# Four 32x32 blocks in place of two masked 64x64 blocks in the level steps of a blocked triangular inverse

## What is computed

```python
def step(S, inp):
    r_t, w_t, k_t, v_t, a_t, b_t = inp
    sa = jnp.einsum('bhvk,bhk->bhv', S, a_t)
    S = S * w_t[:, :, None, :] + sa[..., None] * b_t[:, :, None, :] + v_t[..., None] * k_t[:, :, None, :]
    y = jnp.einsum('bhvk,bhk->bhv', S, r_t)
    return S, y
```

## Time and profile before

| | |
|---|---|
| time, median of 3 runs | 3553.84 us (3550.99 to 3561.1) |
| the profiled execution's own time | 3547.82 us |
| its span, first to last instruction | 3546.0 us |
| `rw_core`, about | 1590 to 2045 us of the span |
| one turn of `m`, about | 57 us |

### The profile page before, as it was taken

One profiled execution on the slowest core, in us unless ns is written; L12 is line 12 of the kernel. 1 busy time (PEld: TensorE's weight loads), 2 busy tenths in 40 slices (PEclk: granted clock), 3 DMA queues, 4 the chain that ended last, 5 costly groups with the idle time before them and its releaser, 6 DMA issues. The chain is left out here.

```text
span 3546.0 us, 61071 instructions
## 1 busy us (share of the span) xinstructions
PE 3405.1 (96%) x25028; PEld 2748.4 (78%) x25028; DVE 1984.6 (56%) x2398; ACT 1194.9 (34%) x1597; POOL 1590.5 (45%) x1148
## 2 busy tenths in 40 slices
PE   7998999999999999999999999999999999999989
PEld 5886778888888777888787877888888887674767
DVE  6886565556224652226767647555542458868452
ACT  4654233333102362226465524333310231242221
POOL 3442377775333323334344425877633323560352
PEclk9998999999999999999999999999999999999999
DMA  2111122224311142241212211222332113111212
GB/s 103 48 49 38 33 87 79 80 89 152 109 42 56 40 179 95 95 147 39 85 46 86 68 37 48 88 89 78 111 128 88 52 42 119 61 48 42 101 43 76
DMA packets 74063, 274.58 MB, mean 77 GB/s; under 512 B 8208, under 2 KB 8592, under 8 KB 73360
## 3 DMA queue, kind: packets, MB, share of 16 engines
q1 hardware_dynamic: 68112, 250.79, 20.8%
q10 hardware_dynamic: 5760, 20.97, 1.5%
HBM read 207.77 MB, written 63.96 MB: 77 GB/s over the span
## 5 line engine op out<-in xcount | busy, mean ns | idle before, releaser
L117 POOL TENSOR_TENSOR gap<-ones 128x1 f32<-128x1 f32 x150 | 46.0, 307 | 1238.8 <-PE ps L167 774.4
L120 POOL TENSOR_TENSOR wlo<-wraw,whi 128x1024 fp32r<-128x1024 f32 (+3 forms) x150 | 391.6, 2611 | 12.5
L893 DVE TENSOR_TENSOR h<-ps,h 128x1024 f32<-128x1024 f32 (+1 forms) x56 | 68.5, 1223 | 288.9 <-PE ps L416 259.6
L167 PE MATMUL ps<-xh,whi 128*128 128x512 f32 x640 | 203.0, 399 | 21.6 <-ACT rw_stage L1888 5.1
L167 PE MATMUL ps<-xl,whi 128*128 128x512 f32 x640 | 199.2, 393 | 0.0
L167 PE MATMUL ps<-xh,wlo 128*128 128x512 f32 x640 | 198.7, 392 | 0.0
L1007 POOL TENSOR_TENSOR wlo<-wraw,whi 128x512 fp32r<-128x512 f32 x126 | 166.3, 1335 | 52.6 <-ACT whi L1130 52.6
L118 POOL TENSOR_SCALAR whi<-wraw 128x1024 fp32r<-128x1024 f32 (+3 forms) x150 | 178.9, 1192 | 0.0
L384 ACT ACTIVATE sq<-h 128x1024 f32<-128x1024 f32 x32 | 34.0, 1061 | 394.1 <-DVE h L893 304.0
L2200 POOL TENSOR_TENSOR rw_levels<-rw_levels,rw_masks 128x512 f32<-128x512 f32 x64 | 87.2, 1378 | 177.2 <-PE ps L2289 140.8
L167 PEld LDWEIGHTS ps<-xh,whi 128*128 128x128 f32 x640 | 119.7, 190 | 56.6 <-issue 8.9
(11 more groups left out here) (673 smaller groups left out, 9535.0 us busy)
## 6 DMA issues: line engine op xcount, KB each, us to landing
wraw<-w_ffn_in SPq DMA_DIRECT2D x88, 512.0 KB, 3.5
ffn_hidden<-sum_of_squares SPq DMA_DIRECT2D x44, 512.0 KB, 2.6
rw_next<-rw_kept SPq DMA_DIRECT2D x40, 512.0 KB, 5.1
wraw<-w_ffn_out SPq DMA_DIRECT2D x32, 512.0 KB, 3.6
ffn_stage<-ffn_hidden SPq DMA_DIRECT2D x30, 512.0 KB, 4.9
rw_kept<-rw_stage SPq DMA_DIRECT2D x24, 512.0 KB, 2.7
rw_kept<-rw_stage ACTq DMA_DIRECT2D x24, 512.0 KB, 2.7
wraw<-w_ple SPq DMA_DIRECT2D x16, 640.0 KB, 3.8
```

Source lines behind the costliest of these rows:

```text
L117: nc.gpsimd.tensor_tensor(g.gap[:, 0:1], g.ones[:, 0:1], g.ones[:, 0:1], ALU.mult)
L120: nc.gpsimd.tensor_tensor(g.wlo[:, s, 0:w], g.wraw[:, s, 0:w], g.whi[:, s, 0:w].bitcast(F32), ALU.subtract).then_inc(g.w_split.sem, 1)
L167: last = nc.tensor.matmul(acc[:, hf, :], w[:, s, c:c + P], x[:, kt, hf * HALF:(hf + 1) * HALF], start=start and kt == 0 and n == 0, stop=s ...
L893: nc.vector.tensor_tensor(ht, flat(banks(g, acc + 2 * s)), ht, ALU.add).then_inc(g.acc_free.sem, 1)
```

## The change

In the levels 2 to 16, every 64x64 matmul becomes two 32x32 matmuls on the array's diagonal. Since a 32-block couples only to itself in these levels, the masks need only 32 columns: the mask work reads `Nc` once and writes 128x256. `Nm` becomes a list of two buffers of that size in the same memory, used in turn, and the mask of a level now waits for the correction of two levels before. `X` is kept 32 columns wide in levels 2 to 16, with one copy instead of two. The last level is as it was. The table of masks shrinks from 834 to 706 columns.

```diff
-NARROW = ["same"] + [f"off{b}" for b in LEVELS] + ["strictT", "inclT", "eye"]
+NARROW = ["same", "strictT", "inclT", "eye"]
 BLOCK_AT = len(NARROW) * CH
-GROUP_AT = BLOCK_AT + 2 * BLK
+GROUP_AT = BLOCK_AT + (2 + len(LEVELS)) * BLK
...
-    Nm = by_tile(level[:, 1, :])
+    Nm = [by_tile(level[:, 1, n * HALF:(n + 1) * HALF]) for n in (0, 1)]
...
-            for lev, b in enumerate(LEVELS):
+            for lev in range(LAST):
                 for h in (0, 1):
-                    if lev == 0:
+                    if lev < 2:
                         pool.wait_ge(g.nc_ready.sem, g.nc_ready.base + m + 1)
                     else:
-                        pool.wait_ge(g.x_done.sem, g.x_done.base + 2 * LEV * m + 2 * (lev - 1) + h + 1)
-                    nc.gpsimd.tensor_tensor(halved(Nm[:, h]), twice(Nc[:, h]), mask_wide(f"off{b}"), ALU.mult).then_inc(g.off_ready.sem, 1)
+                        pool.wait_ge(g.x_done.sem, g.x_done.base + 2 * LEV * m + 2 * (lev - 2) + h + 1)
+                    nc.gpsimd.tensor_tensor(Nm[lev % 2][:, h], Nc[:, h], mask_level(lev), ALU.mult).then_inc(g.off_ready.sem, 1)
...
             for j in range(NT):
-                for rows in heads:
-                    last = nc.tensor.matmul(block_bank(X_BANK + h)[rows, j, :], Nm[rows, h, j, :], DTc[rows, h, j, :], start=True, stop=True)
+                for rows in quarters:
+                    last = nc.tensor.matmul(block_bank(X_BANK + h)[rows, j, :], Nm[lev % 2][rows, h, j, :], DTc[rows, h, j, :], start=True, stop=True)
...
             for j in range(NT):
-                for rows in heads:
-                    last = nc.tensor.matmul(block_bank(D_BANK + h)[rows, j, :], X[rows, h, j, :], D[rows, h, j, :], start=True, stop=True)
+                for rows in quarters:
+                    last = nc.tensor.matmul(block_bank(D_BANK + h)[rows, j, :], X[rows, h, j, 0:BLK], D[rows, h, j, :], start=True, stop=True)
...
         def keep_correction(m, lev, h):
             act.wait_ge(g.x_done.sem, g.x_done.base + 2 * LEV * m + 2 * lev + h + 1)
-            ins = nc.scalar.activation(X[:, h, :, 0:BLK], block_bank(X_BANK + h), ACT.Copy, scale=upper)
             if lev < LAST:
-                ins = nc.scalar.activation(X[:, h, :, BLK:CH], block_bank(X_BANK + h), ACT.Copy, scale=lower)
+                ins = nc.scalar.activation(X[:, h, :, 0:BLK], block_bank(X_BANK + h), ACT.Copy)
+            else:
+                ins = nc.scalar.activation(X[:, h, :, 0:BLK], block_bank(X_BANK + h), ACT.Copy, scale=upper)
             ins.then_inc(g.x_ready.sem, 1)
```

More of the change, by code:

```diff
@@ L1594, in mask_constants @@
     t, s = np.meshgrid(np.arange(P) % CH, np.arange(CH), indexing="ij")
-    off = lambda b: (t // (2 * b) == s // (2 * b)) & (t // b % 2 == 1) & (s // b % 2 == 0)
     m = {"same": t // BLK == s // BLK, "strictT": t < s, "inclT": t <= s, "eye": t == s}
-    m.update({f"off{b}": off(b) for b in LEVELS})
     r, c = np.meshgrid(np.arange(P) % BLK, np.arange(BLK), indexing="ij")
-    block = [(r // 2 == c // 2) & (r % 2 == 1) & (c % 2 == 0), r == c]
+    off = lambda b: (r // (2 * b) == c // (2 * b)) & (r // b % 2 == 1) & (c // b % 2 == 0)
+    block = [off(1), r == c] + [off(b) for b in LEVELS]
     upper = np.arange(P)[:, None] // BLK % 2 == 0
@@ L2084, in rw_core @@
     mask_block = lambda n: mk[:, BLOCK_AT + n * BLK:BLOCK_AT + (n + 1) * BLK].rearrange("p (o s) -> p o s", o=1).broadcast_to([P, 2 * NT, BLK])
+    mask_level = lambda lev: mk[:, BLOCK_AT + (2 + lev) * BLK:BLOCK_AT + (3 + lev) * BLK].rearrange("p (o s) -> p o s", o=1).broadcast_to([P, NT, BLK])
     mask_wide = lambda n: narrow(n).rearrange("p o (a s) -> p o a s", a=2).broadcast_to([P, NT, 2, BLK])
```

## The result

The changed kernel takes 3642.48 us, the median of 5 runs (3637.91 to 3650.37), against 3550.99 us (3550.01 to 3561.1) for the one before: ratio 1.0257, 95% interval 1.0245 to 1.0268. It is 91 us slower; 64 us on the median were forecast, in the range 3576 to 3664. The profiled execution has a span of 3636.9 us. Outside `rw_core` nothing moved: the stretch up to 1590 us and the 1502 us behind the core are as long as before.

What follows compares the result with a forecast made beforehand. TensorE's pace was taken to bound the levels, with instruction fetch binding after the change: 3547.8 + 66 us (8.2 us a turn, 8 turns) = 3614 us profiled. With the median 6 us above, it said 3618 us, range 3576 to 3664.

Steps and rivals of the forecast that it cites:

- What bounds the kernel: TensorE's own pace in the levels; instruction fetch in `outputs` and `gram`, 256 instructions lasting at least about 3.65 us.
- Removals at nothing: One ScalarE copy in 64 places (0.47 us) and half GpSimd's mask work (from 1.38 us) count as nothing.
- Pace of four blocks at once: Array time of a 32x32 level call: 1.0 us at 16 ns a record, or half of that; neither taken.
- Changes of block size: Some 14 changes a turn, about 0.1 us each, 0 to 1.4 us a turn; taken as 0.
- The sum: Per turn, 3.6 us plus 4.6 us added in the two dense level stretches, 8.2 us; 8 turns, 66 us.
- first part: `gram_ar` to `key_sum`: 448 more instructions, 1259 in all, 16.4 us against about 12.8, plus 3.6 us a turn.
- second part: `key_sum`, one call and `variance`, 4.7 us: 144 instructions, less than a block, nothing added.
- third part: Levels 8, 16 and last: 512 more instructions, 1281 in all, 16.6 us against 12.0, plus 4.6 us a turn.
- the upper bound that the prediction gave it: Fetch cost with nothing left of a block at the start and 3.9 us a block: 10 us a turn, 80 in all.
- the rule: Dense stretch: first 128 instructions about 1 us, each block entered 3.65 us, last part some 1.9 us a whole block.
- The clock's rival: Clock falls a level earlier, taking `key_sum` and `variance` with it: up to 32 us more, around 3650 us; chance 0.14.
- The room of 2048 instructions: Would let TensorE hold several blocks in the levels, so fetch doesn't bind: 3506 us; chance 0.07.

Runs made afterwards that it cites:

- `e1_pairs`: Changed kernel with 16 matmuls in place of 32 in each call of levels 2 to 16, same 32x32 blocks, half the products wrong: 3525.5 us, ratio 0.9942.
- `e8_fillall`: Changed kernel with one fp32 128x128 filler matmul on 256 columns ahead of each of the 20 calls of a turn: 3652.6 us, ratio 1.0299.
- `e7_relief`: Kernel before, matmuls untouched, with one ScalarE copy and masks of 32 columns in levels 2 to 16 from the second turn on: 3545.9 us, ratio 0.9982.
- half of the change: Kernel before with `inverses` alone in 32x32 blocks and one ScalarE copy in levels 2 to 16: 3582.7 us, ratio 1.0094.
- `e3_fill`: Changed kernel with two fp32 128x128 filler matmuls on 256 columns ahead of each call of levels 2 and 4: 3646.6 us, ratio 1.0274.
- padding runs: Kernel before with 16 tiny matmuls ahead of each call of levels 2 to 16: on one block 3747.1 us; spread over four blocks 3679.2 us.
- `e10_warm`: Kernel before with one fp32 128x128 filler matmul ahead of each of the last level's four calls a turn: 3552.4 us, ratio 0.9998.
- `e2b_pad4`: Kernel before with 16 tiny matmuls, spread over the four 32x32 diagonal blocks, ahead of each call of levels 2 to 16: 3679.2 us, ratio 1.0356.

## Why the prediction held, and where its sum was small

- **What bounds the kernel.** Right: before, the array's pace and the supply of instructions lie close together in the levels; after, the supply rules. The 123 packets, their distance and the blocks of 256 between rests came as written, and halving the count (`e1_pairs`) took the whole loss away. Putting 88 us of the array's work into seven turns made them 2.5 us shorter (`e8_fillall`), so the array isn't what they wait for in the levels.
- **Removals at nothing.** Right to within 6 us (`e7_relief`).
- **Pace of four blocks at once.** The faster bound: 128 records in 1.46 - 0.19 us, 10 ns each, at full clock. None of it reached the time. Changes of block size cost nothing that shows: the run with half the count has them all and is faster than before.
- **The sum.** The mechanism was right and terms were mis-sized. Mean over the first seven turns, from line to line: first part 12.7 to 17.7 us, plus 5.0 (3.6 forecast); second 4.6 to 5.8, plus 1.2 (0); third 11.9 to 17.4, plus 5.4 (4.6); the rest of the turn minus 0.5 (0). In all 11.2 a turn, 90 us, against 8.2 and 66. The supply's share, 9.9 a turn or 80 us, is the upper bound that the prediction gave it; the 10 us of the second part are the clock's, put at nothing. That both came out at their high side and the sum still lay in the range is the range's width, not the sum's merit. (By its own terms the forecast is 3614 + 6 = 3620 us, not 3618.)
- **Which terms.** A block between two rests lasted 3.76 us in the third part and 3.9 in the first, not 3.65. In the third part the instructions behind the last rest, 167 on average, took 2.4 us, where the rule (1.9 us for a whole block) gives 1.2: they are the last level's, at the low clock. Its start was no worse than forecast: the first rest ended 3.7 us in, after 347 instructions, where the rule gives 4.4. A plain price of 3.65 us for 256 instructions, nothing in hand, fits better than the rule: 1256 instructions 17.9 us (mean 17.7), 1281 18.3 (17.4), half of the change 1000 14.3 (14.1) and 1025 14.6 (14.2), with fillers 1328 18.9 (19.6). By it the change costs (17.9 - 12.7) + (18.3 - 11.9) = 11.6 us a turn, 93 us. It is a fit: a better start and a slower end cancel in it. What lengthens the blocks of the first part was not taken apart.
- **What it says of before.** 12.7 and 11.9 us buy 890 and 835 instructions. The kernel had 811 and 769. The half change, 1003 and 1025, was over the edge already, where my rule saw it on the edge.
- **The clock's rival.** Its event came (PEclk 0.53 before `key_sum`), and a third of its price. `key_sum` took 3.78 us in the second turn, and that is the 1.2 us of the second part, 10 us in all of the rival's 32. The measured time is nearer to its 3650 than to the forecast, but for the supply's sake. With the clock up the whole kernel was not faster (`e3_fill`, `e8_fillall`); that it waits in a supply-bound part for what it gains in front of it is my reading, and the fillers' own work stands beside it.
- **The room of 2048 instructions.** The rests came after single blocks of 256, as above, and the first one of the third part after 201 to 517 instructions in the seven turns. The Trainium skill (Runtime: NRT & Kernel Launch, Instruction fetch mechanics) gives TensorE room for 2048: the runs don't bear that out; its block of 256 they do.

Open: the price of the count alone, free of the clock. Both padding runs changed the clock as well.

## What to carry to other kernels

Count instructions per microsecond, not only busy time: where a stretch of small fp32 matmuls asks for more than about 70 a microsecond on TensorE (18 matmuls of four instructions), splitting a matmul into smaller ones costs time even if the array gets faster by it. A rest that ends by "issue" inside a list without waits, one block of instructions after the last, is the sign. Then a matmul with more moving columns is worth more than one with a better fit. In a stretch that the supply bounds, a higher clock gained nothing here (`e8_fillall`).

## What the runs showed beyond that

- TensorE's instructions came in blocks of 256, and two packets of queue 8 were never less than 3.2 us apart in any trace here.
- The clock: fillers with 128x128 blocks kept it at 2.4 GHz through most of the turns, rests and all (PEclk 0.96 over the levels of `e8_fillall`), but in `e8_fillall` and `e10_warm` it fell behind the last turn, where it had stayed up without them (PEclk 0.64 and 0.56 against 1.00). With tiny matmuls ahead of each call and no rest between, it was at 1.2 GHz (`e2b_pad4`, PEclk 0.50 with PE busy for 8.50 of 8.50 us). A filler that lifts the clock in one place has to be judged by the whole kernel's time.
